# Three columns of each projection made from unscaled tiles behind every norm, and a re-ordered start, LoRA step and decay chain

## What is computed

```python
h = rms_norm(x, norm_mix[0]); x = x + pool_attn_mixer(h, ...)     # norm 0
h = rms_norm(x, norm_ffn[0]); x = x + conv_ffn(h, ...)            # norm 1
h = rms_norm(x, norm_mix[1]); x = x + rglru_mixer(h, ...)         # norm 2
h = rms_norm(x, norm_ffn[1]); x = x + conv_ffn(h, ...)            # norm 3
h = rms_norm_2(x, g) * (1 + scale) + shift; x = x + gate * mixers # norm 4 (rwkv7, spatial gate, conv, s5)
h = rms_norm_2(x, g) * (1 + scale) + shift; x = x + gate * ffn    # norm 5 (relu squared)
out = rms_norm_2(x, final_g)                                      # norm 6
```

## Time and profile before

| | us |
|---|---|
| three executions | 1228.99, 1229.42, 1232.65 |
| median | 1229.42 |
| the profiled execution | 1227.34 |
| its span, first to last instruction | 1225.5 |

### The profile page before, as it was taken

How to read it: one execution, slowest core, us unless ns; L and a number is a source line. 1 busy time by engine, 2 the same in 40 slices (tenths; PEclk the granted TensorE clock), 3 DMA queues, 4 the chain that set the end, 5 groups by cost and what they waited for, 6 DMA issues and landing times.

```text
span 1225.5 us, 20826 instructions
## 1 busy us (share of the span) xinstructions
PE 1104.7 (90%) x8548; PEld 1042.7 (85%) x8548; DVE 863.9 (70%) x1442; ACT 627.7 (51%) x1056; POOL 40.6 (3%) x44
## 2 busy tenths in 40 slices
PE   4997799999968869799999988899999988999996
PEld 3974799999957658799999977789989977999996
DVE  6875788888976687787785464998885576555443
ACT  6444566665544685555564456322224446776441
POOL 0000200000001000000000100000000001000010
PEclk9999899999979899899999988999999988999998
DMA  8436555555542763365666643122333363556650
GB/s 296 128 108 237 188 172 187 184 172 172 195 149 100 244 212 118 119 243 200 246 233 223 214 131 107 44 86 87 106 132 105 120 214 120 191 184 196 185 159 35
DMA packets 59567, 200.40 MB, mean 164 GB/s; under 512 B 6608, under 2 KB 11344, under 8 KB 59216
## 3 DMA queue, kind: packets, MB, share of 16 engines
q1 hardware_dynamic: 57888, 194.54, 48.3%
q10 hardware_dynamic: 1584, 4.53, 1.1%
HBM read 197.99 MB, written 1.05 MB: 162 GB/s over the span
## 4 chain that ended last, share of the span: by engine, by line
PE 71%; DVE 18%; ACT 6%; issue 2%; DMA 2%; SPq 0%; DVEq 0%; ACTq 0%
PE ps L425 71%; DVE wlo L1446 4%; DMA ring<-rg_w_in 1%; ACT whi L955 1%; DVE rq L1629 1%; ACT L955 1%; DVE rst L1475 1%; DVE xr L1452 1%; ACT L L955 1%; DVE raw L1446 1%; DVE sc L1801 1%; DVE w L1446 1%; DVE xr L1811 0%; DVE raw L1452 0%; DVE cosT L1446 0%
## 5 line engine op out<-in xcount | busy, mean ns | idle before, releaser
L425 PE MATMUL ps<-hh,whi 128*128 128x256 f32 x1656 | 490.1, 296 | 49.4 <-DVE hl L1446 30.8
L425 PE MATMUL ps<-hl,whi 128*128 128x256 f32 x1656 | 478.6, 289 | 0.0
L425 PE MATMUL ps<-hh,wlo 128*128 128x256 f32 x1656 | 478.3, 289 | 0.0
L1446 DVE TENSOR_TENSOR wlo<-ring,whi 128x1024 fp32r<-128x1024 f32 (+1 forms) x313 | 375.1, 1211 | 72.5 <-ACT whi L955 71.7
L425 PEld LDWEIGHTS ps<-hh,whi 128*128 128x128 f32 x1656 | 328.1, 198 | 71.8 <-issue 42.9
L955 ACT ACTIVATE whi<-ring 128x1024 fp32r<-128x1024 f32 (+1 forms) x313 | 321.5, 1039 | 105.1 <-PE ps L425 62.6
L425 PEld LDWEIGHTS ps<-hl,whi 128*128 128x128 f32 x1656 | 328.6, 198 | 1.4 <-issue 1.0
L425 PEld LDWEIGHTS ps<-hh,wlo 128*128 128x128 f32 x1656 | 327.9, 198 | 0.0
L425 PE MATMUL ps<-hidh,whi 128*128 128x256 f32 x608 | 170.3, 280 | 0.0
L425 PE MATMUL ps<-hidl,whi 128*128 128x256 f32 x608 | 170.1, 280 | 0.0
L425 PE MATMUL ps<-hidh,wlo 128*128 128x256 f32 x608 | 170.1, 280 | 0.0
(11 more groups left out here) (318 smaller groups left out, 1336.2 us busy)
## 6 DMA issues: line engine op xcount, KB each, us to landing
ring<-ffn_w_in SPq DMA_DIRECT2D x88, 512.0 KB, 3.9
ring<-ffn_w SPq DMA_DIRECT2D x64, 512.0 KB, 4.1
ring<-w_in SPq DMA_DIRECT2D x51, 512.0 KB, 3.7
ring<-ada_w SPq DMA_DIRECT2D x48, 512.0 KB, 5.5
ring<-ffn_w_out SPq DMA_DIRECT2D x32, 448.0 KB, 4.5
ring<-rg_w_in SPq DMA_DIRECT2D x20, 512.0 KB, 4.6
ring<-pa_w_in SPq DMA_DIRECT2D x16, 512.0 KB, 5.2
ring<-ffn_w_out SPq DMA_DIRECT2D x16, 512.0 KB, 4.0
```

Of the source, the lines that this page charges most:

```text
L425: return e.matmul(o, l, r, start=start, stop=stop)
L1446: return e.tensor_tensor(o, a, b, op)
```

## The change

- **early(n)** on TensorE makes the first three columns of the projection (EARLY[n]) from unscaled tiles hh, hl of x * g, k by k with three banks open; the sum of squares is made after its second k. project then goes on from scaled tiles. For norms 4 and 5 two more columns of hh and hl hold the shift, so that its product comes out as column 256.
- **high_of_h, low_of_h** make those unscaled tiles inside the residual, one pair for each column of x.
- **h_tiles** now contains stats and overwrites hh and hl with the scaled ones. hh of k waits until the early columns have read it (plain; for k = 7 the end of the early columns). Weight splits stand between the tiles (feed at k = 3 and 6 on ScalarE, at 5 and 8 on VectorE).
- **lift** multiplies the three early results by rst into SBUF (qk, zl, xl, zz, or At and Rt), and adds the shift for norms 4 and 5; what reads a column reads there.
- At the start, vec is first on SP's queue; ScalarE casts eight tiles, then weight splits stand between the squares. The sigmoid comes behind five splits, and the three transfers of attention come before the root.
- The head norms stand later (HEAD_NORMS), the r and i matmuls too (RI).
- decay() is split in two and moved to columns 2 and 4 of the residual of layer 0, its exp to column 3; the modulation step of ADA_OUT goes into the columns of the second conv FFN, and gsc is made at column 0 of its residual.
- The LoRA step is split: tanh and sigmoid after column 1, the matmuls after columns 4 and 5; columns 17 and 18 follow.
- The five transfers of mixers and the one of rglru are issued before the root on ScalarE.
- The output leaves in eight transfers.

```diff
-ADA_IN = ((), (2, 5, 8, 11, 14, 17, 20))
-ADA_OUT = ((), (2,))
+ADA_IN = ((), (2, 5, 8, 11, 14, 17, 19, 21))
 ADA_PA = (3, 4, 5, 6, 7, 8, 9)
 ADA_RG = ((5, 7, 9), (1, 3, 5, 7, 8))
 YW = ((0, 2), (2, 2), (4, 2), (6, 4))
+
+
+
+EARLY = [
+    [("pa_w_in", 4), ("pa_w_in", 5), ("pa_w_in", 6)],
+    [("ffn_w_in0", 0), ("ffn_w_in0", 22), ("ffn_w_in0", 1)],
+    [("rg_w_in", 10), ("rg_w_in", 11), ("rg_w_in", 12)],
+    [("ffn_w_in1", 0), ("ffn_w_in1", 22), ("ffn_w_in1", 1)],
+    [("w_in", 6), ("w_in", 2), ("w_in", 3)],
+    [("ffn_w1", 0), ("ffn_w1", 1), ("ffn_w1", 2)],
+]
+
+
+
+HEAD_NORMS = {8: (), 9: (), 10: (0, 1), 11: (2, 3), 12: (4,), 13: (5,), 14: (6,), 15: (7,)}
+RI = ((), (), (), (), (), (), (0, 1), (2, 3), (4, 5), (6,), (7,), (8,), (9,)) + ((),) * 7
 
 
 def weight_order():
@@ -120,8 +135,6 @@
...
-    6, 2, 3, 0, 1, 4, 5, 17, 18,
-    "R", 7, 8, "R", 9, 10, "R", 11, "G", "R", 12, 13, "G", "R", 14, 15, 16, "G", "S", "R", "G", (0, 2),
+    6, 2, 3, 0, 1, "R", 4, 5, "R", 17, 18, 7, 8, "R", 9, 10, "R", 11, "G", "R", 12, 13, "G", "R", 14, 15, 16, "G", "S", "R", "G", (0, 2),
...
+            def early(n):
+
+                c = width(n)
+                outs = [take(at)[:, 0:c] for at in EARLY[n]]
+                for k in range(8):
+                    hlow.wait_ge(e, (n, k))
+                    for (w, m), o in zip(EARLY[n], outs):
+                        at = tail(w, m)
+                        low.wait_ge(e, at)
+                        j = turn[at] % NS
+                        mm(o, whi[j][:, k, :], hh[:, k, 0:c], k == 0, False)
+                        mm(o, whi[j][:, k, :], hl[:, k, 0:c], False, False)
+                        t = mm(o, wlo[j][:, k, :], hh[:, k, 0:c], False, k == 7)
+                        if k == 7:
+                            t.then_inc(*through.up(at))
+                    if k < 7:
+                        t.then_inc(*plain.up((n, k)))
+                    if k == 1:
+                        stats(n)
...
+                early(0)
+                for i in range(3):
+                    give(("pa_w_in", 4 + i), at_dve, ("lift", i))
+                for ms in ([7, 8], [9], [10], [11], [12], [13], [14], [15]):
                     project("pa_w_in", ms, 0)
-                    at += [m - 4 for m in ms]
-                    while len(at) > 1:
-                        head_norm(at.pop(0))
-                for m in range(12, 16):
...
+                early(n)
+                for i, at in enumerate(EARLY[n]):
+                    give(at, ff_dve, (l, "lift", i))
+                project(w, [23, 2], n)
+                give((w, 23), ff_dve, (l, "g", 1))
+                give((w, 2), ff_dve, (l, "u", 2))
...
+                    for i in RI[m]:
...
+            def high_of_h(n, m):
+
+                last_h = {1: ("pa_w_in", 3), 2: ("ffn_w_in0", 43), 3: ("rg_w_in", 9), 4: ("ffn_w_in1", 43), 5: ("w_in", 26)}
+                if n and m == 0:
+                    through.wait_ge(e, tail(*last_h[n]))
+                    if n > 3:
+                        ada_dve.wait_ge(e, "gsc")
+                        sh = mod[:, 24 * (n - 4):24 * (n - 4) + 8].unsqueeze(2).to_broadcast([128, 8, 2])
+                        act(hh[:, :, T:T + 2], sh, ACT.Copy).then_inc(*hhigh.up((n, "shift")))
+                act(hh[:, m, 0:T], x[:, m, :], ACT.Copy, gain(n, m)).then_inc(*hhigh.up((n, m)))
...
+                stats(n)
                 for k in range(8):
                     scaled.wait_ge(e, (n, k))
                     r = raw[k % 4][:, :]
                     if n > 3:
-                        ada_dve.wait_ge(e, "gsc")
                         act(r, r, ACT.Identity, gsc[:, n - 4, k:k + 1], mod[:, 24 * (n - 4) + k:24 * (n - 4) + k + 1]).then_inc(*modded.up((n, k)))
                         modded.wait_ge(e, (n, k))
-                    act(hh[:, k, :], r, ACT.Copy).then_inc(*hhigh.up((n, k)))
+                    if k < 7:
+                        plain.wait_ge(e, (n, k))
+                    else:
+                        through.wait_ge(e, tail(*EARLY[n][2]))
+                    act(hh[:, k, 0:T], r, ACT.Copy).then_inc(*hhigh.up((n, "scaled", k)))
+                    if k in (3, 6):
...
+                        if n < 6:
+                            high_of_h(n, m)
+                if n < 6:
+                    feed(first(n))
...
+                def square_of(i):
+                    if i > 3:
+                        at_pe.wait_ge(e, ("hn", i - 4))
+                    if i < 3:
+                        at_dve.wait_ge(e, ("lift", i))
+                    src = qk[:, i, :] if i < 3 else out_of("pa_w_in", 4 + i)
+                    act(sq[:, i % 4, :], src, ACT.Square).then_inc(*at_act.up(("sq", i)))
+
+                h_tiles(0)
+                for i in range(3):
+                    square_of(i)
+                for ms in ([7, 8], [9], [10], [11], [12], [13], [14], [15]):
...
+                    if l == 0 and m == 3:
+                        rg_dve.wait_ge(e, "c1")
+                        act(cfr[1], cfr[1], ACT.Exp).then_inc(*rg_act.up("c1"))
...
-            e.dma_start(vec[:, :], d["vec"]).then_inc(*vecs_in.up("vec", 16))
-            e.dma_start(cst[:, 0:384], d["cst"][:, 0:384]).then_inc(*vecs_in.up("all", 16))
+            e.dma_start(cst[:, 0:384], d["cst"][:, 0:384]).then_inc(*ones_in.up("all", 16))
+            vecs_in.wait_ge(e, "all")
             for m in range(8):
                 xin[m].wait_ge(e, m)
+                high_of_h(0, m)
+            feed(-4)
+            for m in range(4):
                 gather(0, m)
-            vecs_in.wait_ge(e, "all")
+            feed(-2)
+            for m in range(4, 8):
+                gather(0, m)
+            feed(first(0))
             act(cpar[15], P("c", 0, 8), ACT.Sigmoid).then_inc(*ada_act.up("sig"))
-            stats(0)
...
+            def low_of_h(n, m):
+
+                if n > 3 and m == 0:
+                    sh = mod[:, 24 * (n - 4):24 * (n - 4) + 8].unsqueeze(2).to_broadcast([128, 8, 2])
+                    hhigh.wait_ge(e, (n, "shift"))
+                    low_of(hl[:, :, T:T + 2], sh, hh[:, :, T:T + 2]).then_inc(*hlow.up((n, "shift")))
+                hhigh.wait_ge(e, (n, m))
+                stt(hl[:, m, 0:T], x[:, m, :], gain(n, m), hh[:, m, 0:T].bitcast(F32), MUL, SUB).then_inc(*hlow.up((n, m)))
+
             def h_tiles(n):
+
+                stats(n)
                 mean.wait_ge(e, ("rst", n))
                 for k in range(10):
                     if k < 8:
                         r = raw[k % 4][:, :]
                         if k > 3:
-                            hlow.wait_ge(e, (n, k - 4))
+                            hlow.wait_ge(e, (n, "scaled", k - 4))
                         if n < 4:
-                            g = P(("norm_mix0", "norm_ffn0", "norm_mix1", "norm_ffn1")[n], k)
-                            stt(r, x[:, k, :], g, rst[:, :], MUL, MUL).then_inc(*scaled.up((n, k)))
+                            stt(r, x[:, k, :], gain(n, k), rst[:, :], MUL, MUL).then_inc(*scaled.up((n, k)))
                         else:
                             tt(r, x[:, k, :], rst[:, :], MUL).then_inc(*scaled.up((n, k)))
                     if k >= 2:
                         q = k - 2
-                        hhigh.wait_ge(e, (n, q))
-                        low_of(hl[:, q, :], raw[q % 4][:, :], hh[:, q, :]).then_inc(*hlow.up((n, q)))
+                        hhigh.wait_ge(e, (n, "scaled", q))
+                        low_of(hl[:, q, 0:T], raw[q % 4][:, :], hh[:, q, 0:T]).then_inc(*hlow.up((n, "scaled", q)))
+                    if k in (5, 8):
+                        feed(first(n) + k // 3 + 1)
+
+            def lift(o, n, i):
+
+                w, m = EARLY[n][i]
+                p = out_of(w, m)
+                if n > 3:
+                    e.tensor_copy(shw[:, i:i + 1], ps[where[w, m]][:, T:T + 1]).then_inc(*shifted.up((n, i)))
+                return tt(o, p, rst[:, :], MUL)
 
             def add_to_x(n, m, p):
                 if n < 5:
...
+                    if i > 1:
+                        at_dve.wait_ge(e, ("qk", i - 2))
...
+            def decay():
+                c = cfr
+                lam = P("rg_lam", 0, 10)
+                ts(c[0], lam, -1.0, 0.0, MUL, MAX).then_inc(*rg_dve.up("c0"))
+                ts(c[1], lam, -1.0, None, MUL).then_inc(*rg_dve.up("c1"))
+                rg_dve.wait_ge(e)
+                tt(c[1], c[1], lam, MIN).then_inc(*rg_dve.up("c1"))
+                yield
+                rg_act.wait_ge(e, "c1")
...
+                    if l == 0 and m in (2, 4):
+                        next(decays)
+                    if l == 1 and m == 0:
+                        for n, nm in enumerate(("norm_mix2", "norm_ffn2")):
+                            ada_dve.wait_ge(e)
+                            stt(gsc[:, n, :], mod[:, 24 * n + 8:24 * n + 16], 1.0, P(nm, 0, 8), ADD, MUL).then_inc(*ada_dve.up("gsc"))
...
+                            if m:
+                                low_of_h(3, m - 1)
```

(30 more changed lines are left out.)

317 lines of the change are left out of this document (142 added, 175 removed).

## The result

The changed kernel is slower by 0.4%: 1235.51 us in the median (1232.34 to 1238.64) against 1229.51 us for the kernel before, a ratio of 1.0044 with a 95% interval of 1.0026 to 1.0062. The forecast was 1217.7 us, 1201 to 1232. The profiled execution took 1236.74 us, its span is 1234.9 us (before 1225.5).

The account below looks back on a forecast made before the run. TensorE was taken to set the pace of most of the span, VectorE in head norms and second residual. Gains 5.5 + 4.5 + 10 + 1 + 0.5 + 1.7 less 11.5 at the start, 11.7 us: median 1217.7, range 1201 to 1232.

Parts of the forecast that it names:

- Early columns at norms 1 and 5: Conv FFN 0 and ffn_w1: three columns from unscaled tiles fill TensorE's wait, gaining 5.5 and 4.5 us.
- time at which five columns are done: Measure used per norm, from the residual's last matmul; at norm 1, 22.0 us before and 16.3 after.
- Norm 4: Mixers: gain 8.4 us from early columns plus 2 us of the LoRA wait, together 10 us.
- given back: Rival at 1229 us, chance 0.11: late weight splits and the 1.2 GHz level behind early blocks take the gains back.
- Second residual and norm 2: Layer 0's residual and recurrent mixer, moved decay included: net gain 0.5 us, anything from -6 to +6.
- the price of the moved decay: Second residual: 10.8 us more for VectorE, which has no slack, so TensorE ends 9.3 us later.
- The slower rival: Rival at 1238 us, chance 0.09: VectorE's second residual decides, its 9.3 us not won back, start at -14, norm 3 at -3.
- that sum is 70.4. To it come waits: Start: VectorE's work from the reciprocal on, plus waits, ends head 7 at about 76 us; cost 11.5 us.
- the stall of 7 us: Norm 3: TensorE waits about 7 us at the first k, for a weight split behind the adds and low casts.
- five columns at 517.6 against 518.8: Norm 3: trace times at which five columns end, after and before, counted as a gain of 1 us.
- The signs: Trace checks, such as no low-half activation wait above 4 us, first matmul near 11 us, attention not starting before 70 us.
- The rival of the drain behind table loads: Rival at 1223 us, chance 0.02: four table loads on the path cost 5.5 us more, by the Trainium skill's page.

Follow-up runs that it names:

- e1_aligned: The changed kernel with 32 unused bytes behind dmy, so later tiles start where they did in the kernel before, modulo 128 bytes: ratio 0.9985.
- e4_decay: The changed kernel with the second half of decay() moved back behind the third x column of the recurrent mixer: ratio 1.0048.
- e2_start: The changed kernel with norm 0 as before (no early columns, casts or splits ahead of the root; old head-norm order and transfers): 1211.34 us, ratio 0.9835.
- e3_norm3: The changed kernel with norm 3 as before (no early columns, lift, added casts or splits between scaled tiles there): ratio 1.0002.
- e7_heads: The changed kernel with the head norms two columns earlier (HEAD_NORMS edited), all else the same: ratio 0.9979.
- e11_feed3: The changed kernel with VectorE's due weight split ahead of the eight adds to x at the recurrent mixer's end: ratio 1.0019.
- e5_shift: The kernel before with 32 unused bytes behind dmy and nothing else, putting residual inputs at 96 modulo 128 bytes: ratio 0.9954.
- e8_both: The changed kernel with norms 0 and 3 as before and 32 unused bytes behind dmy: 1198.94 us, ratio 0.9758.
- e6_hh: The kernel before with 32 unused bytes ahead of hh and 96 behind hl, putting both at 64 modulo 128 bytes: ratio 0.9953.
- e9_all96: The kernel before with unused bytes putting hh, hl and the residual inputs at 96 modulo 128, weight tiles still at 32: ratio 0.9843.
- e10_weights: The kernel before with unused bytes putting only the weight tiles at 96 modulo 128 bytes in place of 32: ratio 0.9909.
- e12_best: The changed kernel, norms 0 and 3 as before, with hh, hl rows and residual inputs at 96 modulo 128, lo in sc32: 1192.55 us, ratio 0.9694.

## Why the prediction was wrong

- **Early columns at norms 1 and 5**: right, 5.9 and 4.3 us for 5.5 and 4.5. The count "time at which five columns are done" held: at norm 1 it is 22.2 us before and 16.5 after (forecast 22.0 and 16.3), at norm 5 22.9 and 17.9. The clock stayed at 1.00 behind both.
- **Norm 4**: 10.6 us for 10, but by luck. Five columns are done 21.5 us behind the residual, where the count had 17.9 (before 26.2, forecast 26.3): a gain of 4.8, not 8.4. TensorE waits 3.16 us for a weight split behind the early columns and is then at the 1.2 GHz level, the very thing that the rival "given back" described. The forecast had 2 us for the LoRA step, and it gave more: its wait fell from 4.02 to 0.72 us, its twelve matmuls take 2.58 us for 3.77, and nine columns with the LoRA step are done at 36.4 us for 45.5.
- **Second residual and norm 2**: the price of the moved decay came out right in size (9.5 us for 9.3), in part by luck. The wait is 5.67 us; about 2.5 more go to the half clock behind it, and up to 1.4 to the slower matmuls (528 x 2.6 ns; e1_aligned, without these, gets 0.6 us back in the stage). Neither of the last two was in the sum. The 9.5 us are won back and 3.5 us more. The net gain of 3.9 lies inside the -6 to +6 of the forecast, and e4_decay shows that the decay's own share in it is nothing. The slower rival had the right side and nearly the time (1238), but the wrong mechanism: it lived on these 9.3 us not being won back. Only its loss at norm 3 (-3, measured -5.4) and a dearer start (-14, measured -26.6) came true.
- **The start**: the step "that sum is 70.4. To it come waits" failed. It summed VectorE's work and added waits for ScalarE. It took TensorE to be free because it begins earlier (at 11 us; measured 13.8). The waits listed there add up to 76.7, not 76, a small slip. What is missing in it is that moving the head norms back also keeps the banks of their columns longer. After the four waits that TensorE has there (2.99, 5.00, 3.27 and 4.28 us) it runs partly or wholly at the 1.2 GHz level, which makes the next head wait in turn. Of the 15 us missed, 8.3 are in the head norms (about 1.5 the root, 2 ScalarE's waits, 5 TensorE). Some 3.6 more go between the heads and the last projection, where the first scores and one column take 4.1 us longer at a mean clock of 0.54. The rest, 3.1 us, lies between the last projection and the end of residual 1 (59.1 us for 55.9). It stands in e2_start too (2.6), so it does not belong to norm 0. It is hardly more than profiles differ there: 57.1 to 59.1 us in e3_norm3, e4_decay, e7_heads and e11_feed3, and 57.7 in e5_shift, which has the old code. Of the 26 us, e7_heads shows 8 to be the place of the head norms; how the other 18 divide among the later root, the banks and the clock stays open.
- **Norm 3**: the stall of 7 us was forecast, and measured at 6.7. The step that failed is "five columns at 517.6 against 518.8". Counted from the residual's end that is 24.5 us against 25.7; measured are 27.6 against 26.0, a loss of 1.6 us in place of a gain of 1. Ahead of the fifth column stands a second wait for a weight split, 2.25 us, with the 1.2 GHz level behind it (the granted clock is 0.50 from 530.60 to 534.00), and neither is in the count. The third, 1.90 us, stands behind the sixth column, and the stage loses 5.4 us in all. e11_feed3 takes the stall away and keeps waits of 2.10 and 1.91 us: VectorE's splits stay late, so the count must run until its queue is empty.
- **Residuals at a slower pitch**: the sum had no term for them, that is, it took untouched products to cost the same; that failed. 2256 matmuls x 2.6 ns = 5.9 us; e1_aligned gave 7 back. No row ahead of the run shows this cause, but rows could have: in the kernel before two kinds of product of equal size had two pitches, 117.4 and 119.9 ns.
- **The end** gave 1.3 for 1.7.
- **The signs**: the longest wait for hl is 2.3 us, as forecast, and no wait for a split above 0.98 us stands in the first ten columns of conv FFN 0. The first reciprocal (24.6 us for 23), head 7's (ends at 83.8 for 75), the first matmul (13.8 for 11), the gap in the second residual (5.67 for 9) and the clock behind norm 4 (0.53 in the 7.2 us shown) came out otherwise.
- The rival of the drain behind table loads has no support: in the changed kernel the table load at 21.31 us ends at 22.59, and the activation behind it starts at 22.61.

e8_both shows what the change is worth without the three: 30 us of gain over the kernel before. Where the forecast had a gain or a loss for a stage, its direction was right in all but norm 3.

## What to carry to other kernels

Before work is put ahead of a root, count what every engine has to do before that root, and what PSUM banks stay occupied by what is now later. At norm 0, where short chains run through three engines, the early start of TensorE gained nothing here. Take each norm by itself: by the stages four of six profited, and the other two gave more back than the four won. A stage that comes out as forecast still wants its parts compared: at norm 4 two errors cancelled. And after any edit of the allocations compare the start-to-start times of matmuls that were not touched.

## What the runs showed of the hardware

The time between the starts of two 128x256 float32r matmuls, with TensorE busy without a gap at a granted clock of 1.00, by the starts of moving and weight tiles modulo 128 bytes:

| kernel, product | moving | weights | distance | ns |
|---|---|---|---|---|
| before, projections | 32 | 32 | 0 | 119.9 |
| after, residuals | 32 | 32 | 0 | 120.0 |
| before, residuals | 64 | 32 | 32 | 117.4 |
| e1_aligned, residuals | 64 | 32 | 32 | 116.7 |
| e6_hh, projections | 64 | 32 | 32 | 118.1 |
| e5_shift, residuals | 96 | 32 | 64 | 113.5 |
| e9_all96, projections | 96 | 32 | 64 | 113.4 or 117.8 |
| e10_weights, projections | 32 | 96 | 64 | 113.4 or 117.8 |
| e12_best, projections | 96 | 32 | 64 | 115.4 to 119.2, mean 117.1 |
| e10_weights, residuals | 64 | 96 | 96 | 118.3 |
| after, mgh and mgl | 0 | 32 | 96 | 120.0 |
| after, projections | 32 to 88 (hh), 96 to 152 (hl) | 32 | 0 to 56, 64 to 120 | 115.7 to 128.3, mean 119.8 |

Distance 0 is at 120 ns in its two rows, 6% above the best (the few products of mgh, also at distance 0, are at 120.0 in the kernel before and at 118.7 in e1_aligned). In e9_all96 and e10_weights the value holds over most of a stage; in e12_best it wanders. What picks between the values at distance 64 is open; the 11 us between the executions of e9_all96 may be the same thing. That these reads disturb each other is my reading and was only argued; what is shown is that moving the weight tiles alone changes the pitch. The distance modulo 128 bytes is not the whole rule. In the last row, the changed kernel's own projections, each row of hh and hl starts 1032 bytes behind the one before, so every k has another distance. A matmul then takes from 115.7 to 128.3 ns by its place among the 24 of a column, the same in all 29 columns from 200 to 285 us. None is at 113.5, though for hl the distances begin at 64, and the mean is that of the kernel before.

The Trainium skill (TensorE: Matmul & The Clock Gate, Step-by-step: what each phase is for) says that TensorE reads moving data and weights through two ports, and that loading the next weights takes no read bandwidth from the running matmul. By that, e10_weights should have changed nothing; the measurement decides, and it gained 0.9%.
